# Column groups, packed samples and a reordered stream in a two-layer recurrent decoder step

## The chip, the cores and the metric

The kernel runs on one core of one Trainium2 chip, in one launch. The metric is the device time of that launch in microseconds, the median of several runs. The host only lays the arrays out.

## The reference

One inference step of a trunk of two layers (`DEPTH = 2`) for a prompt of 512 tokens and for 8 sample sequences of 4 tokens each, with the same weights. D_MODEL is 1024; there are 4 heads with keys and values of width 128; everything is float32.

```python
for l in range(DEPTH):
    mod = (silu(c) @ w_ada[l] + b_ada[l])              # 9 sequences x 6 * 1024: shifts, scales, gates
    h = rmsnorm(x, norm_mix[l]) * (1 + sc_m) + sh_m
    mix = token_mixers(h)                               # below
    x = x + gt_m * mix
    h = rmsnorm(x, norm_ffn[l]) * (1 + sc_f) + sh_f
    x = x + gt_f * swiglu(h)
y = rmsnorm(x, final_norm)

# token_mixers: one input projection, three branches of 4 heads, each with a 128 x 128 state a head
# A gated DeltaNet: width-4 causal convolution, SiLU, l2-normed q and k, per-head decay,
#   a triangular solve in each chunk; output rmsnorm, times silu(z)
# B retention: rotary q and k, fixed decays; output less its mean, divided by its deviation, times silu(g)
# C HGRN2: per-channel forget gate; output rmsnorm, times sigmoid(g)
# each branch projected to 1024, merged by sigmoid gates, and one output projection
```

The outputs are y for both groups and the new states of all branches and sequences.

## The kernel before

**Layout.** The 544 tokens (512 of the prompt, 32 of the samples) are columns, in two halves of 272: 256 prompt columns and 16 sample columns each. Features are on partitions.

**The stream.** The weights of all projections come as *slabs* of 128 output columns, in one order that `stream()` writes out by hand: rows, 12 convolution tiles, 8 rope tiles (q and k of retention), ret_v, gdn_z, ret_g, the gates and branches of the merge with the HGRN2 tiles between, output projection, feed-forward. Each slab is split by GpSimd (lines 600 and 602) into a high and a low part. A *k-step* (`k_tile`, line 627) is six TensorE matmuls: three products of parts, for two halves. A tile is 8 k-steps (branch tiles 4). Results go to two alternating PSUM buffers (`gemm_psum`), and ScalarE or VectorE works them off.

**Fills.** All small work runs between k-steps. Every engine walks through the same program with its own `Feed`: where TensorE's program has `fill(n, limit)`, n k-steps are issued, and ScalarE's and VectorE's programs have the same call, in which they work off the tiles that those steps complete. `drain(limit)` does the rest up to a limit (`Z_END`, `RG_END`, `M0_END` and so on). Each engine runs its program strictly in order. SyncE issues all transfers, in order too; it runs some slabs ahead.

**Conditioning.** The first 2 x 1024 columns of w_ada come as four groups of 2 MB; `silu_c` (9 columns) is the stationary operand, 512 columns stream, and 16 transposes turn the result (lines 769, 774). The other 32 tiles are computed in the convolution part with the weights as the stationary operand and 9 moving columns (`ada_tile`, line 790), three tiles per convolution tile (`ADA_STEPS`), from 4 buffers (`ADA_SLOTS`).

**Norms of heads.** `square_sum` (line 669) sums squares over partitions with a one-hot stationary operand of 8 columns into 8 rows; ScalarE takes the root, VectorE the reciprocal (`rows_of`, line 1231), and `spread` (line 678) spreads each row back over 128 partitions with 8-row weights; VectorE multiplies a tile at a time (line 1311 or 1405).

**Chunks and samples.** Each branch takes the prompt in four chunks of 128 tokens, in two pairs for gated delta, and then the samples (`c == NCH`), which have their own shapes: 32 columns a head. `gdn_level` does one of seven levels of the triangular inverse for a pair of chunks: masked columns on VectorE (`gdn_columns`), a fill, a second product (line 851), VectorE's additions (`gdn_add`, line 1491), transposes (line 858). `LEVEL_FILL` sets the k-steps in a level. For the samples, `sample_outputs` reads the 8 x 4 states with one matmul for each state (lines 703, 723: 8 or 4 moving columns), and `sample_states` makes the state updates from 32-row operands, a head at a time (line 735), which VectorE adds (line 1371). `out_norm` strings these together at the end of each branch: sums, two heads' states, spreads, the other two heads' states.

**Semaphores.** PSUM has four more banks (`mix_psum`) for the small work. `acquire(b)` waits until bank b is free, and VectorE or ScalarE releases it.

## Time and profile before

| | |
|---|---|
| median of 3 runs | 3214.1 us (3212.15 to 3222.64) |
| profiled execution | 3212.13 us |
| its span, first to last instruction | 3210.2 us |
| TensorE matmul busy | 2922.2 us, 91%, 20570 recorded |
| TensorE weight loads busy | 2681.7 us, 84% |
| VectorE, ScalarE, GpSimd busy | 1228.9, 472.3, 1400.5 us |
| mean granted TensorE clock | 0.903 of 2.4 GHz |
| bytes moved by DMA | 264.11 MB, 82 GB/s on average |

A matmul's busy time overlaps that of its neighbours, so that the mean duration of one is longer than what it adds; busy time of a group divided by its count is nearer to that. Line 1725 is the helper through which ScalarE records most of its work. "[idle before <-X]" is the time that an engine stood still before a row, and what ended it. Layer 0 runs from about 18 to 1605 us, and layer 1 repeats it.

### The profile page before, as it was taken

The numbers are of one execution on the slowest core, as the hardware profiler recorded it, in microseconds if no ns is written. First come the engines' busy times: TensorE is split into PE (matmuls) and PEld (weight loads), VectorE is DVE, ScalarE is ACT, GpSimd is POOL, SyncE is SP. The second block draws the span as 40 slices with busy tenths as digits, with TensorE's granted clock in tenths as the row PEclk, the third lists the DMA queues.
The fourth block names the chain that finished last, engine by engine and source line by source line (L and its number), as shares of the span: only waits on it lengthen the run. The fifth ranks groups of instructions, "written<-read, shape, count | busy, mean of one in ns | idle before, by whom it ended". The sixth has DMA issues, their size and how long they took to land. (4 is left out here: it accounts for less than half of the span.)

```text
span 3210.2 us, 48470 instructions
## 1 busy us (share of the span) xinstructions
PE 2922.2 (91%) x20570; PEld 2681.7 (84%) x20570; DVE 1228.9 (38%) x1572; ACT 472.3 (15%) x944; POOL 1400.5 (44%) x728
## 2 busy tenths in 40 slices
PE   6998998889998879999889989989899988799997
PEld 3977896877995879999859779968689968799996
DVE  2545412313353384333235444132225335732332
ACT  2221122111112110000023111221110121100000
POOL 1322232343533547776523222313355336477774
PEclk9987897986997989999999789969889979899998
DMA  7520011211411312222275100112113113122222
GB/s 276 183 88 27 27 47 40 83 56 40 121 45 43 114 60 91 83 91 85 63 266 172 57 27 28 53 50 59 56 60 112 47 37 127 60 90 82 93 80 74
DMA packets 126319, 264.11 MB, mean 82 GB/s; under 512 B 9616, under 2 KB 68496, under 8 KB 124304
## 3 DMA queue, kind: packets, MB, share of 16 engines
q1 hardware_dynamic: 126096, 260.93, 25.5%
q8 instruction: 165, 2.70, 0.3%
q14 instruction: 58, 0.48, 0.0%
HBM read 239.72 MB, written 21.17 MB: 81 GB/s over the span
## 5 line engine op out<-in xcount | busy, mean ns | idle before, releaser
L627 PE MATMUL gemm_psum<-h_hi_lo,w_hi_lo 128*128 128x272 f32 x12000 | 1710.9, 302 | 66.2 <-DVE h_hi_lo L1114 38.8
L627 PEld LDWEIGHTS gemm_psum<-h_hi_lo,w_hi_lo 128*128 128x128 f32 x12000 | 1619.4, 199 | 176.7 <-issue 139.8
L600 POOL TENSOR_TENSOR w_hi_lo<-w_raw,consts 128x1024 fp32r<-128x1024 f32 (+3 forms) x362 | 617.4, 1706 | 1744.5 <-PE gemm_psum L627 1618.8
L602 POOL TENSOR_TENSOR w_hi_lo<-w_raw,w_hi_lo 128x1024 fp32r<-128x1024 f32 (+3 forms) x362 | 784.0, 2166 | 28.4
L1725 ACT ACTIVATE tiles<-gemm_psum 128x544 f32<-128x544 f32 (+1 forms) x188 | 116.3, 623 | 1304.8 <-PE gemm_psum L627 1303.6
L627 PE MATMUL gemm_psum<-ffn_hi_lo,w_hi_lo 128*128 128x272 f32 x2112 | 266.8, 288 | 0.0
L627 PEld LDWEIGHTS gemm_psum<-ffn_hi_lo,w_hi_lo 128*128 128x128 f32 x2112 | 266.4, 188 | 0.0
L627 PE MATMUL gemm_psum<-o_hi_lo,w_hi_lo 128*128 128x272 f32 x1152 | 161.0, 296 | 16.3 <-POOL w_hi_lo L602 16.3
L627 PEld LDWEIGHTS gemm_psum<-o_hi_lo,w_hi_lo 128*128 128x128 f32 x1152 | 152.4, 194 | 18.1 <-POOL w_hi_lo L602 17.4
L1708 DVE TENSOR_TENSOR tiles<-gemm_psum,tiles 128x544 f32<-128x544 f32 x44 | 31.9, 725 | 319.6 <-PE gemm_psum L627 319.6
L1714 DVE TENSOR_TENSOR ffn_hi_lo<-tiles,ffn_hi_lo 128x544 fp32r<-128x544 f32 x44 | 119.8, 2722 | 1.5
L790 PEld LDWEIGHTS mix_psum<-silu_c,tiles 128*128 128x128 f32 x1024 | 120.1, 192 | 0.0
L790 PE MATMUL mix_psum<-silu_c,tiles 128*128 128x9 f32 x1024 | 118.3, 252 | 0.0
L1275 DVE SCALAR_TENSOR_TENSOR scratch<-scratch,params 128x568 f32<-128x568 f32 x72 | 102.1, 1418 | 2.6
L678 PE MATMUL mix_psum<-rows,consts 8*128 8x272 f32 x160 | 82.5, 667 | 21.1 <-DVEq L1057 21.1
L1725 ACT ACTIVATE scratch<-mix_psum 128x512 f32<-128x512 f32 (+3 forms) x90 | 48.5, 562 | 313.7 <-PE mix_psum L858 222.0
L1126 DVE TENSOR_TENSOR gated_sample<-gemm_psum,mod 128x32 f32<-128x32 f32 x48 | 9.2, 192 | 201.7 <-PE gemm_psum L627 201.7
L735 PE MATMUL mix_psum<-tiles 32*128 32x512 f32 x64 | 61.3, 1054 | 23.9 <-ACT tiles L1725 23.9
L1273 DVE TENSOR_SCALAR scratch<-scratch,params 128x568 f32<-128x568 f32 x24 | 30.8, 1283 | 132.6 <-ACT scratch L1725 132.2
L678 PEld LDWEIGHTS mix_psum<-rows,consts 8*128 8x128 f32 x160 | 45.0, 308 | 40.3 <-DVEq L1057 23.0
L1169 DVE TENSOR_TENSOR tiles<-gemm_psum,tiles 128x544 f32<-128x544 f32 x32 | 23.0, 718 | 139.7 <-PE gemm_psum L627 139.7
L1725 ACT ACT_TABLE_LOAD x44 | 56.5, 1283 | 123.3 <-issue 83.3
(225 smaller groups left out, 2413.2 us busy)
## 6 DMA issues: line engine op xcount, KB each, us to landing
w_raw<-in_w_gu SPq DMA_DIRECT2D x88, 512.0 KB, 3.5
tiles<-in_w_ada SPq DMA_DIRECT2D x64, 512.0 KB, 4.1
w_raw<-in_w_merge SPq DMA_DIRECT2D x48, 384.0 KB, 3.0
w_raw<-in_w_first SPq DMA_DIRECT2D x34, 512.0 KB, 3.6
w_raw<-in_w_ret SPq DMA_DIRECT2D x32, 512.0 KB, 3.4
w_raw<-in_w_hg SPq DMA_DIRECT2D x32, 512.0 KB, 3.5
w_raw<-in_w_merge SPq DMA_DIRECT2D x48, 256.0 KB, 2.7
w_raw<-in_w_dn SPq DMA_DIRECT2D x32, 384.0 KB, 3.1
```

The source lines that it names most:

```text
L600: pool.tensor_tensor(hi, src, ones[:, 0:1].broadcast_to([P, words]), ALU.mult).then_inc(hi_done, 1)
L602: pool.tensor_tensor(lo, src, hi.bitcast(F32), ALU.subtract).then_inc(split_done, 1)
L627: mm = pe.matmul(GP[:, 2 * (tile % 2) + h, 0:HALF], whl[:, n % 2, a, j * P:(j + 1) * P], rhs[:, b, step, h * HALF:(h + 1) * HALF], start=s ...
L678: pe.matmul(B[:, b, 0:HALF], sel[0:8, i, :], RWO[0:8, h * HALF:(h + 1) * HALF], start=True, stop=True).then_inc(full[b], 1)
L735: pe.matmul(B[:, 2 + half, :], ke[0:SW, h, :], UM[n][h % 2][0:SW, 4 * half:4 * half + 4, :], start=True, stop=True).then_inc(full[2 + half ...
L790: mm = pe.matmul(B[:, 2, j * NJ:(j + 1) * NJ], w[:, kk, :], CS[:, kk, :], start=kk == 0, stop=kk == KD - 1)
L1169: k.link(dve.tensor_tensor(halves(dst), gp(tile), halves(sg), ALU.mult))
L1273: ins = dve.tensor_scalar(co[:, 0:COW], xin, wt, None, ALU.mult)
L1275: ins = dve.scalar_tensor_tensor(out=co[:, 0:COW], in0=xin, scalar=wt, in1=co[:, 0:COW], op0=ALU.mult, op1=ALU.add)
L1708: k.link(dve.tensor_tensor(halves(FT[:, 1, :]), gp(tile), halves(FT[:, 0, :]), ALU.mult))
L1714: k.link(dve.tensor_tensor(AH[:, 1, i, :], FT[:, 1, :], AH[:, 0, i, :].bitcast(F32), ALU.subtract))
L1725: return act.activation(out, in_, func, **kw)
```

## The change

**Conditioning in column groups.** `silu_c` is padded with zeros to 32 columns. `conditioned` writes the eight products of a tile to four groups of 32 PSUM partitions in turn, which are four column groups of the array, with the weights as the moving operand. For the four first groups and for the 32 later tiles the four partial results of each group are copied to SBUF by ScalarE (`ada_copy`, three tiles at a time) and summed and turned by one product with a constant (`join`; `ada_join`). `ADA_SLOTS` is 7, of which 3 are loaded only after the first norm is done.

**Sums and spreads.** `four_sums` has 32-column one-hot weights, four heads in four column groups; `four_spreads` has 32-row weights, four heads in four row groups, one half of the tokens at a time, into four banks. VectorE multiplies four heads of one half at a time. The scale of q moves from `rows_of` into that product.

**Packed samples.** The 4 x 32 sample columns of the heads are one set of 128 columns: `nh` is 1 instead of 4 heads of 32, and masks keep the heads and sequences apart. `read_states` has the 32 columns of a head as the stationary operand and streams four states (512 columns), four heads in four column groups; ScalarE copies that to SBUF, and `pick` takes the right columns out with eight products of 16 moving columns. `sample_states` does four heads at a time in four row groups.

**Order.** gdn_z comes before ret_v in the stream, and `Z_END` lies before ret_v. `LEVEL_FILL` is (1, 1, 1). VectorE's additions come before the fills in `gdn_level`. In `out_norm` all sums, the root and the spreads come before all state updates. Buffers move accordingly (`sq_l2`, `sq_o`, `swap_temp`, `UM`, `QS`).

```diff
-LEVEL_FILL = (2, 1, 1)
-GATE_TURN = 10
+LEVEL_FILL = (1, 1, 1)
+GATE_TURN = 11
...
+    block("gdn_z", "first", 13, 4)
     block("ret_v", "ret", 8, 4)
-    block("gdn_z", "first", 13, 4)
     block("ret_g", "ret", 12, 4)
...
-Z_END = BASE["ret_g"]
+Z_END = BASE["ret_v"]
...
-    ADA_SLOTS = 4
+    ADA_SLOTS = 7
+    ADA_EARLY = 4
...
-    ADA_STEPS = (1, 4, 6)
+    ADA_STEPS = (3, 5, 6)
...
+                    if n == 0:
+                        sp.wait_ge(sig("h_ready"), KD)
+                        for j in range(ADA_EARLY, ADA_SLOTS):
+                            load_ada(j)
...
+                def four_sums(sq, j, first, last):
+
+                    if first:
+                        acquire(0)
+                        acquire(1)
+                    k.next(sig("square_ready"), H)
                     for h in range(2):
...
+                        for i in range(H):
+                            mm = pe.matmul(B[32 * i:32 * i + 32, h, 0:HALF], hot[:, j, :], sq[i][:, h * HALF:(h + 1) * HALF],
+                                           start=first, stop=last, skip_group_check=True)
+                    if last:
+                        mm.then_inc(sig("sums_done"), 1)
+
+                def four_spreads(j, half):
+
+                    for i in range(H):
+                        acquire(i)
+                        pe.matmul(B[:, i, 0:HALF], spr[32 * i:32 * i + 32, j, :],
+                                  RWO[32 * i:32 * i + 32, half * HALF:(half + 1) * HALF], start=True, stop=True
+                                  ).then_inc(full[i], 1)
...
+                def read_states(bank, queries):
+
+                    for half in range(2):
+                        acquire(bank + half)
+                        for h in range(H):
+                            mm = pe.matmul(B[32 * h:32 * h + 32, bank + half, :], queries[:, h * SW:(h + 1) * SW],
+                                           S8[:, h, 4 * half:4 * half + 4, :], start=True, stop=True, skip_group_check=True)
+                        mm.then_inc(full[bank + half], 1)
+
+                def pick(out, read, fresh):
+
+                    o4 = out.rearrange("p (h b t) -> p h b t", h=H, b=NS)
+                    for b in range(NS):
+                        mm = pe.matmul(o4[:, :, b, :], read[:, b, :], pick_seq[:, :, b, :], start=fresh,
+                                       stop=fresh or b == NS - 1, skip_group_check=True)
+                    return mm
...
-                def sample_states(n, h, limit):
+                    read_states(0, flat(0))
+                    fill(3, limit)
+                    k.peek(free[0])
+                    k.peek(free[1])
+                    acquire(2)
+                    pe.matmul(hcol(2, 0), val, sc, start=True, stop=False, skip_group_check=True)
+                    pick(hcol(2, 0), QS[n][0], False).then_inc(full[2], 1)
+
+                def sample_states(n, half):
 
                     ke = (small, rsm, hsm)[n]["kend"]
-                    k.next(sig("masked_values"))
-                    for half in range(2):
-                        acquire(2 + half)
-                        pe.matmul(B[:, 2 + half, :], ke[0:SW, h, :], UM[n][h % 2][0:SW, 4 * half:4 * half + 4, :],
-                                  start=True, stop=True).then_inc(full[2 + half], 1)
-                        fill(1, limit)
+                    if half == 0:
+                        k.next(sig("masked_values"))
+                    for h in range(H):
+                        p0 = 32 * h
+                        acquire(h)
+                        pe.matmul(B[:, h, :], ke[p0:p0 + 32, 0, :], UM[n][p0:p0 + 32, 4 * half:4 * half + 4, :],
+                                  start=True, stop=True).then_inc(full[h], 1)
...
-                    for i in range(H):
-                        square_sum(i, H, hot[:, i, :], 8, sq_o[n])
-                        fill(1, limit)
-                    for h in range(2):
-                        sample_states(n, h, limit)
+                    fill(2, limit)
+                    four_sums(sq_o[n], 0, True, True)
+                    fill(3, limit)
                     k.next(sig("rows_ready"))
-                    for i in range(H):
-                        spread(i, i)
+                    for half in range(2):
+                        four_spreads(0, half)
                         fill(2, limit)
-                    for h in range(2, H):
-                        sample_states(n, h, limit)
-
+                    fill(1, limit)
+                    for half in range(2):
+                        sample_states(n, half)
+                        fill(4, limit)
+
+
+                def conditioned(bank, at, w):
+                    for kk in range(KD):
+                        p0 = 32 * (kk % 4)
+                        mm = pe.matmul(B[p0:p0 + 32, bank, at], CS[:, kk, :], w[:, kk, :], start=kk < 4, stop=kk >= 4,
+                                       skip_group_check=True)
+                    return mm
...
+                def ada_join(g):
+                    k.next(sig("ada_lot_copied"))
+                    if g == 0:
+                        acquire(2)
+                    for j in range(g * ADA_LOT, min((g + 1) * ADA_LOT, 4 * KD)):
+                        o = j % ADA_LOT * P
+                        mm = pe.matmul(B[:, 2, j * NJ:(j + 1) * NJ], ada_part[g % 2][:, o:o + P], join, start=True, stop=True)
+                    mm.then_inc(sig("ada_lot_joined"), 1)
...
                 def gdn_level(chunks, lv, limit):
                     for c in chunks:
                         gdn_columns(c, lv)
-                    fill(LEVEL_FILL[0], limit)
                     if lv:
                         for c in chunks:
                             gdn_add(c, lv)
+                    fill(LEVEL_FILL[0], limit)
+                    if lv:
                         fill(LEVEL_FILL[1], limit)
                     fill(LEVEL_FILL[2], limit)
...
+                def ada_copy(g):
+                    count = min(ADA_LOT, 4 * KD - g * ADA_LOT)
+                    act.wait_ge(sig("ada_used"), g * ADA_LOT + count)
+                    if g >= 2:
+                        act.wait_ge(sig("ada_lot_joined"), g - 1)
+                    k.link(f(ada_part[g % 2][:, 0:count * P], B[:, 3, 0:count * P], ACT.Copy))
```

## Rows read from the trace of the kernel before

**Rows 1.** The page: TensorE's busy time, and its granted clock in 40 slices.

```profile
PE 2922.2 (91%) x20570; PEld 2681.7 (84%) x20570; DVE 1228.9 (38%) x1572; ACT 472.3 (15%) x944; POOL 1400.5 (44%) x728
...
PEclk9987897986997989999999789969889979899998
```

**Rows 2.** Line 627 (projections) by stretch, layer 0: busy (count), clock, DMA share, GB/s.

```profile
20.80:64.70 43.90, 0.01 (x1) 0.04 (x1) 0.97 0.76 300
74.90:213.60 138.70, 81.46 (x572) 73.55 (x571) 1.00 0.47 156
222.00:254.90 32.90, 16.16 (x60) 13.92 (x60) 0.50 0.05 17
254.90:465.80 210.90, 95.70 (x590) 83.86 (x590) 0.91 0.10 31
479.50:515.70 36.20, 18.53 (x116) 16.12 (x115) 0.86 0.13 42
515.70:573.80 58.10, 20.46 (x90) 17.29 (x90) 0.62 0.17 48
632.30:691.70 59.40, 40.84 (x301) 39.55 (x300) 0.91 0.19 58
691.70:772.00 80.30, 38.92 (x164) 33.58 (x165) 0.62 0.10 30
772.00:849.20 77.20, 77.20 (x618) 77.19 (x617) 1.00 0.27 84
949.80:980.20 30.40, 16.84 (x122) 16.47 (x121) 0.83 0.21 61
980.20:1048.50 68.30, 32.35 (x156) 27.95 (x155) 0.70 0.12 35
```

**Rows 3.** TensorE by line and form, both layers: count, busy us, mean duration in ns.

```profile
L678 PE MATMUL mix_psum<-rows,consts 8*128 8x272 f32 x160 | 82.5, 667 | 21.1 <-DVEq L1057 21.1
L735 PE MATMUL mix_psum<-tiles 32*128 32x512 f32 x64 | 61.3, 1054 | 23.9 <-ACT tiles L1725 23.9
...
L723 PE MATMUL mix_psum<-sample_cols,x 128*128 128x4 f32 x256 | 43.1, 300 | 0.0
...
L769 PE MATMUL mix_psum<-tiles,silu_c 128*9 128x512 f32 x64 | 27.8, 592 | 0.0
...
L703 PE MATMUL mix_psum<-scratch,x 128*128 128x8 f32 x128 | 22.0, 309 | 0.0
...
L669 PE MATMUL mix_psum<-tiles,consts 128*8 128x272 f32 x48 | 14.0, 417 | 2.5 <-ACT tiles L1725 2.5
```

**Rows 4.** All engines while the first conditioning weights arrive.

```profile
30.00:40.00 10.00, 10.00 (x26) 2.17 (x25) 8.40 (x9) 1.86 (x3) 0.00 (x0) 1.00 1.04 418
```

**Rows 5.** DMA issues by line: count, KB each, median us to landing.

```profile
scratch<-in_w_ada_first SPq DMA_DIRECT2D x4, 2048.0 KB, 19.4
```

**Rows 6.** TensorE in order of time, in the convolution stretch.

```profile
79.69 1.85 PE L790 MATMUL mix_psum<-silu_c,tiles 128*128 128x9 f32 x16
81.39 1.75 PE L627 MATMUL gemm_psum<-h_hi_lo,w_hi_lo 128*128 128x272 f32 x12
```

**Rows 7.** TensorE by line, 259 to 262 us.

```profile
L823 PE MATMUL mix_psum<-scratch,consts 4*128 4x128 f32 x32 | 2.8, 283 | 0.0
```

**Rows 8.** Order of time, a level of the first gated-delta pair.

```profile
287.80 2.89 DVE L1148 TENSOR_TENSOR tiles<-tiles,consts 128x544 f32<-128x544 f32 x1
...
291.83 1.97 PE L858 MATMUL mix_psum<-consts,scratch 128*128 128x128 f32 x8 [3.60 <-DVE scratch L1491]
```

**Rows 9.** VectorE by line and form, both layers.

```profile
L1275 DVE SCALAR_TENSOR_TENSOR scratch<-scratch,params 128x568 f32<-128x568 f32 x72 | 102.1, 1418 | 2.6
...
L1231 DVE RECIPROCAL rows<-rows 8x544 f32<-8x544 f32 x8 | 28.3, 3539 | 2.9 <-DVE x L1371 2.0 <-DVE x L1366 1.0
...
L1371 DVE SCALAR_TENSOR_TENSOR x<-x,scratch,mix_psum 128x128 f32<-128x128 f32 x64 | 18.0, 343 | 49.0 <-PE mix_psum L735 49.0
...
L1311 DVE TENSOR_TENSOR tiles<-mix_psum,tiles 128x544 f32<-128x544 f32 x16 | 11.6, 724 | 34.7 <-PE mix_psum L678 34.0 <-DVE tiles L1311 0.6
```

More of the change, by code:

```diff
@@ L1357, in sample_outputs, with sample_states @@
                     release(2)
[L1359 to L1360 removed]
+                def sample_states(n, half):
+                    if half == 0:
                         k.next(sig("states_landed"), 16 * H)
[L1362 to L1363 removed]
+                    eg = flat(12) if n == 2 else small["eg"][:, 0, :]
+                    for h in range(H):
+                        k.next(full[h])
                         if n == 1:
```

595 lines of the change are left out of this document (322 added, 273 removed).

## The prediction

> **What bounds the kernel.** I read the page first: TensorE is busy 91% of the span, no other engine over 44%, and the clock row dips wherever TensorE's share dips [rows 1]. So the sum is TensorE's, and what matters is which of its time is not the projections. I then asked for the projections alone (line 627), stretch by stretch through the first layer [rows 2]. The reader is to see the stretch from 772.0 to 849.2 us: nothing but projections, 77.2 us for 616 to 618 matmuls, 0.1255 us each at the full granted clock (2.4 GHz). With that price every other stretch splits into projections (count x 0.1255) and a rest: small products, waits, and projections at the half clock (1.2 GHz). The rests, in us: start 43.8; convolution 138.7 - 71.8 = 66.9; spreading of the norms 32.9 - 7.5 = 25.4; gated-delta pairs 210.9 - 74.0 = 137; their samples 21.6; the three output norms 46.8, 59.7, 48.7; the stretches with the retention and HGRN2 sample outputs 21.6 and 15.1. The projections themselves do not change, so the change is worth what it takes out of these rests, twice (the second layer repeats the first). The small products are priced by [rows 3], dividing busy time by count; each fp32 product is two recorded matmuls (a conditioning tile of eight calls shows x16 [rows 6]).
>
> **Start.** Four groups of conditioning weights, in all 64 recorded 512-column matmuls a layer, of 0.434 us each (27.8/64 [rows 3]), 27.8 us. Serial on one column group, that is 30.4 to 57.6. With the eight products dealt to four column groups, 7 us of work remain, and the weights decide: transfers ran at 418 GB/s [rows 4], the late groups landed a median 19.4 us after issue [rows 5], which from issues near 20 us puts the last at 40 to 43 us. Then 1.8 us of products, the copy 0.6, and 16 joining products with 128-column weights, 32 x 0.106 = 3.4 us (6.8 at the half clock) where 1.1 us of 9-row ones stood. The first projection comes near 55.5 instead of 64.7: **9 us** (serial: -2.5; at best 11).
>
> **Convolution.** An old conditioning tile is 16 recorded matmuls, 1.70 us from its start to the next projection [rows 6]; 32 of them 54.4 us, the eight sums of squares some 8 (32 recorded of 0.25 to 0.29 [rows 3]), and 4.5 is left. A new tile streams 128 columns with 32-column weights. Bounds: one column group after another costs the 1.76 us of 16 x 0.11 as 128-column products do; four at once 0.43. I take 0.65, since small matmuls are not issued endlessly close (an estimate). Adding 11 joins of 0.85 (64 x 0.106 and the switch) and two packed sums of 1.2: 4.5 + 20.8 + 9.4 + 2.4 = 37, so 66.9 becomes 37; the reciprocal without its scaling pass takes 1.5 us from the wait at the end. **31 us** (serial -13; best 37). What runs beside it: VectorE's four convolution passes, 4 x 1.42 = 5.7 us a tile [rows 9], under 8.7 us a tile on TensorE; ScalarE gets a 0.6 us copy; SyncE must bring 2 MB per tile, 240 GB/s, where this stretch moved 156 [rows 2] and 418 was reached [rows 4]. Seven slots give the transfers two tiles of lead.
>
> **Do packed products overlap?** Nothing here packs columns. But the gate products (line 823, four rows, at partitions 0 and then 32) pack rows by accident: 32 recorded matmuls in 2.8 us [rows 7], 0.088 each, where 128 columns cost 0.106 on a single group: at each change of row group the next group's begin before the last ones end. So row groups do run at the same time in fp32; for columns it is an inference.
> The Trainium skill, "TensorE: Matmul & The Clock Gate", Part 3, states that both overlap, 2.38x for three column tiles and 3.07x for four row tiles; no run here shows the column figure. At 2.38/3 of ideal a tile would cost 0.54 us instead of 0.65, 4 us a layer better.
>
> **Spreading.** Eight spreads with 8-row weights, 2.1 us each at the half clock, alternate with eight pairs of k-steps at half clock: 0.50 granted throughout [rows 2, 3]. New: four rounds of four row-packed products, 1.1 us at half clock (0.5 at full), and VectorE's multiply of 1,088 columns, 1.45 us (twice 0.724 [rows 9]). Its first rope tile (4.3 us: 2.89 for the sine product [rows 8] and two passes of 0.72) now falls between the third and fourth multiply, so the branch starts some 18.5 us after the first spread, not 33. **14 us** (4 to 20).
>
> **Gated-delta pairs.** VectorE worked off a rope tile between the masked columns and the additions; TensorE's transposes waited 3.60 us for the additions, then ran at the half clock [rows 8]. Four such waits and their slow stretches cost about 28 us of the 137; 888 other matmuls x 0.107 = 95 are unchanged. The additions now come first, so rope delays only the next level's columns, 5 us away. By counting k-steps (one fill less per level, ret_v moved behind gdn_z): rope 1 at step 16 stalls as before, 2 at step 24 and 7 at step 64 end in the last fill and still cost 4 + 3 each, 3 costs 2 to 3, the others nothing. SiLU of gdn_z puts table loads before ScalarE's copies, 3 us. **8 us** (-10 to 25).
>
> **Samples of gated delta.** State reads load 128-column weights for 8 moving columns, 64 recorded, 11 us a layer [rows 3], over 12 with the value products between. New: 16 products of 512 moving columns in column groups, 3.4 us (14 serial), 16 picks 3.4, and small products of 0.22 instead of 0.4 to 1.0. Four ScalarE copies of 0.6 lie under the fill. The drain of 18 k-steps ahead moves behind, so turn and gates meet VectorE cold: 2 us of wait. 21.6 becomes 15: **7 us** (-4 to 10). Retention and HGRN2, 43.1/4 = 10.8 us of reads each [rows 3] and 2 more of value products and slow clock, become 1.7 + 1.9: **19.5 us** for both (9.5 to 21).
>
> **Output norms.** The old order let VectorE do two heads' states before the 3.54 us reciprocal [rows 9], so spreads waited 4 us, eight 32-row state products took 0.96 [rows 3] at the half clock (16 recorded, 15 us), four spreads 8.4, four sums 4 to 5, and the k-steps between ran slow; the first norm also ran out of projections (4.9 us idle). New rest of norm 0: wait for four squares 0.5, sums 1.1, wait for root and reciprocal 2.4 (4.7 less three k-steps), two spread rounds 1.1, two state rounds 1.9, a wait for VectorE's 16 state updates of about 0.28 (duration 0.343 [rows 9], overlapping) before the second round 4.5, slow clock and switches 4.5: 16. Norm 1 adds 3.2 for its means and 4 where VectorE meets hg_f's forget gate: 24. Norm 2: 20. Gains 31 + 36 + 29 = **96 us** (60 to 108).
>
> **Sum.** 9 + 31 + 14 + 8 + 7 + 19.5 + 96 = 184.5 a layer, 369 in all. The profiled execution took 3212.1 us (span 3210.2), 0.1% under the median 3214.1. Forecast 2843, say **2845**; its own range, from the bounds that belong to overlapping groups, 2790 to 2890.
>
> **Rivals.**
> *Column groups do not overlap.* They still stream at full pace: 0.18 instead of 0.07 us for each of 720 recorded matmuls a layer, 81 us back, 3005. For it: no row shows them; against: row groups do. Chance 0.12.
> *Half overlap, or transfers bound the convolution.* Two at a time costs 35 us a layer, 2914. If the conditioning weights come no faster than this stretch's 156 GB/s, its 30 us go, 2905. Against: 418 was reached. Together 0.12.
> *The half clock stays.* If short packed groups between k-steps hold 1.2 GHz as the old norms do (0.62 [rows 2]), 20 k-steps a norm cost 15 instead of 4 us more, and the spreading 6: 39 a layer, 2922. Against: TensorE's unfilled share falls. Chance 0.12.
> *Slower: every column-group matmul pays its whole duration,* because the array empties between groups. At 0.283, 0.417 and 0.592 us by width [rows 3, 7] that is 0.35 on average, 203 us a layer more than I charge: 3249. It decides from 0.33 us a matmul on. Against: the sums of squares, eight-column weights between k-steps, cost 0.29 us a recorded matmul with their changes [rows 3], not their duration 0.417; streaming takes 0.227, so a change costs some 0.1. Chance 0.03.
> The Trainium skill, "TensorEngine Tiling (Array Packing)", Key Properties, says that changing the tiling mode drains TensorE; at the 0.1 us a change derived above it is inside my terms, once per matmul it is this rival.
>
> **Chances.** Forecast 0.55; the three middle rivals 0.36; slower 0.03; no change 0.01, if the waits merely move to VectorE; below 2790 0.05. Runs here tell 0.3% from no change. Range 2790 to 2960: out are slower, no change, the low tail and most of the serial case. Faster 0.96, same 0.01, slower 0.03.
>
> **What will show it.** Conditioning products starting in fours within some ns, a tile in 0.5 to 0.7 us; the first projection near 55 us; convolution rest near 37; the clock row above 0.93; norm stretches with rests of 16 to 24 and VectorE's state updates as the releaser before the second state round. Wrong if tiles take 1.7 us (serial), if TensorE waits for `tiles` transfers, or if the waits for line 1491's additions stay at 3.6 us.

## The result, and the profile after

The changed kernel took **2858.1 us** (median of 4 runs, 2855.1 to 2862.8) against 3214.2 for the kernel before on the same chip; the ratio is 0.8889, 95% interval 0.8868 to 0.8910. The forecast was 2845 (2790 to 2960), faster. The profiled execution took 2855.1 us, 357.0 less than that of before, where the sum of the prediction had 369.

The page first: TensorE's busy time and its granted clock, as in [rows 1].

```profile
PE 2567.6 (90%) x20358; PEld 2443.5 (86%) x20358; DVE 1224.0 (43%) x1537; ACT 442.8 (16%) x824; POOL 1402.6 (49%) x728
...
PEclk8998999999998989999979898999999998999998
```

TensorE lost 355 us of busy time with only 212 fewer recorded matmuls, 1% of them: what went is duration, not count. VectorE's busy time hardly moved (1228.9 to 1224.0). The clock row has fewer dips; the mean over the span is 0.946.

Next the projections alone (line 668 after, 627 before), by stretch of the first layer. Columns: stretch, its length, busy time (count), granted clock, DMA share, GB/s. They answer to [rows 2].

```profile
20.80:61.50 40.70, 0.00 (x0) 0.81 0.84 331
73.60:178.40 104.80, 81.79 (x566) 1.00 0.58 197
184.50:202.90 18.40, 9.68 (x60) 0.87 0.14 44
202.90:403.40 200.50, 82.30 (x504) 0.92 0.09 27
403.40:432.90 29.50, 21.45 (x138) 0.94 0.15 40
432.90:481.70 48.80, 35.95 (x259) 0.93 0.23 73
591.30:630.00 38.70, 25.67 (x172) 0.96 0.23 62
833.60:870.00 36.40, 20.68 (x133) 0.81 0.15 44
630.00:695.00 65.00, 65.00 (x521) 1.00 0.30 90
```

The last row gives the same price as before, 65.00/521 = 0.125 us. The first norm now covers itself with 259 projections at clock 0.93, where [rows 2] had 90 at 0.62.

To compare the layers, both traces were cut at the same events of TensorE (first projection, first spread, first transpose of the branch, first gate product of the samples, first sum of squares of a norm) and count x 0.1255 us of projections taken off each piece. What is left is the rest, in us per first layer:

| piece | rest before | rest after | gain | forecast |
|---|---|---|---|---|
| start, to the first projection | 64.7 | 61.55 | 3.2 | 9 |
| convolution, to the first spread | 77.6 | 43.3 | 34.3 | 31 |
| spreading | 25.5 | 10.9 | 14.6 | 14 |
| gated-delta pairs | 136.9 | 137.2 | -0.3 | 8 |
| samples of gated delta | 22 | 12 | 10 | 7 |
| retention and HGRN2 with their sample outputs | | | 19.6 | 19.5 |
| output norms 0, 1, 2 | 46.9, 59.7, 45.8 | 16.5, 17.0, 19.7 | 99 | 96 |

The pieces sum to 180. From projection 4200 on the two traces stay 179.4 us apart until the layer ends; the forecast was 184.5, and the second layer gave 177. The start's two figures include idle time that both kernels have. The stretches of retention and HGRN2 were not tested by a run of their own; in the trace the state reads of retention, which with their value products took TensorE 11.9 us in the kernel before (637.0 to 648.9 us), have become reads of 1.9 and picks of 1.7 us, near the forecast (1.7 and 1.9).

The new and changed products by form, both layers (count | busy us, mean ns | idle before, releaser), beside [rows 3].

```profile
L828 PE MATMUL mix_psum<-tiles,silu_c 128*32 128x128 f32 x1024 | 41.3, 279 | 0.0
...
L731 PE MATMUL mix_psum<-rows,consts 32*128 32x272 f32 x160 | 21.0, 539 | 19.7 <-DVEq L1146 17.1 <-DVEq L1141 2.5
L799 PE MATMUL mix_psum<-tiles 32*128 32x512 f32 x64 | 19.5, 739 | 3.9 <-DVEq L1141 3.8
...
L828 PE MATMUL mix_psum<-scratch,silu_c 128*32 128x512 f32 x64 | 11.9, 883 | 12.5 <-DMA scratch<-in_w_ada_first 12.5
...
L749 PE MATMUL mix_psum<-x,sample_cols 128*32 128x512 f32 x64 | 7.7, 598 | 0.0
```

The column-group products of a tile have a mean duration of 279 ns each, but 1,024 of them occupy only 41.3 us, 40 ns apiece: they lie over one another. One tile in order of time:

```profile
75.96 0.64 PE L828 MATMUL mix_psum<-tiles,silu_c 128*32 128x128 f32 x16
76.54 1.01 PE L668 MATMUL gemm_psum<-h_hi_lo,w_hi_lo 128*128 128x272 f32 x6
```

Sixteen recorded matmuls in 0.58 us from the first one's start to the next projection, against 1.70 in [rows 6]. Each break in the projections for a tile costs another 0.19 us (6 of them take 0.94 us instead of 0.75); the breaks for the old tiles cost 0.09 (12 take 1.60 us instead of 1.51).

### The profile page after: what moved, and what is told of

It is laid out like the page before. It is cut to its first block and busy times, and to the rows that moved or that the text cites. A ratio compares the mean times of both kernels' runs of the same rounds, so it can differ in the third digit from the quotient of the medians.

```text
span 2853.3 us, 47939 instructions
## 1 busy us (share of the span) xinstructions
PE 2567.6 (90%) x20358; PEld 2443.5 (86%) x20358; DVE 1224.0 (43%) x1537; ACT 442.8 (16%) x824; POOL 1402.6 (49%) x728
## 5 line engine op out<-in xcount | busy, mean ns | idle before, releaser
L668 PE MATMUL gemm_psum<-h_hi_lo,w_hi_lo 128*128 128x272 f32 x12000 | 1638.3, 296 | 75.5 <-DVE h_hi_lo L1203 46.7
L668 PEld LDWEIGHTS gemm_psum<-h_hi_lo,w_hi_lo 128*128 128x128 f32 x12000 | 1566.1, 194 | 127.5 <-issue 90.5
L668 PEld LDWEIGHTS gemm_psum<-o_hi_lo,w_hi_lo 128*128 128x128 f32 x1152 | 150.8, 192 | 20.2 <-POOL w_hi_lo L643 19.9
L1833 ACT ACTIVATE scratch<-mix_psum 128x512 f32<-128x512 f32 (+3 forms) x112 | 59.2, 547 | 410.1 <-PE mix_psum L947 196.6
L1833 ACT ACTIVATE tiles<-mix_psum 128x512 f32<-128x512 f32 (+1 forms) x78 | 43.6, 573 | 219.4 <-PE mix_psum L740 98.5
L940 PE MATMUL mix_psum<-scratch 128*128 128x64 f32 x388 | 51.5, 290 | 16.9 <-DVE scratch L1584 16.9
L1425 DVE COPY sample_cols<-tiles 128x128 f32<-128x128 f32 x20 | 9.5, 533 | 132.4 <-ACT tiles L1833 87.0
L940 PEld LDWEIGHTS mix_psum<-scratch 128*128 128x128 f32 x388 | 50.2, 208 | 18.2 <-DVE scratch L1584 18.2
L1218 DVE TENSOR_TENSOR x<-x,gated_sample 128x32 f32<-128x32 f32 x48 | 58.9, 1227 | 1.6
```

The lines of the kernel that those rows point to most:

```text
L668: mm = pe.matmul(GP[:, 2 * (tile % 2) + h, 0:HALF], whl[:, n % 2, a, j * P:(j + 1) * P], rhs[:, b, step, h * HALF:(h + 1) * HALF], start=s ...
L940: per_head(b0 + 1, lambda h: pe.matmul(columns(b0 + 1, h), t["u"][:, h, :], t["x"][:, h, :].rearrange("p (n t) -> p n t", t=m), start=True ...
L1218: k.link(dve.tensor_tensor(sample(xi), sample(xi), SCT[:, :].rearrange("p (a b) -> p a b", a=2), ALU.add))
L1425: k.link(dve.tensor_copy(SMP[:, at * H:(at + 1) * H, :].rearrange("p i (a b) -> p i a b", a=2), brt[:, src:src + H, :].rearrange("p i (a b ...
L1833: return act.activation(out, in_, func, **kw)
```

## Experiments

Times are medians; the ratio is to the kernel before, with its 95% interval. The changed kernel stands at 2858.1, ratio 0.8889 (0.8868 to 0.8910). In the diffs minus is the changed kernel. The rests below are cut at the same events in all kernels, norm 0 to the first projection of the next stage and norm 1 from 12 us ahead of its sums, so they stand 1 to 2 us above those of the table; among kernels that leave a norm and the fills alone they differ by 1 to 2 us (norm 0 18.3 to 20.3, norm 2 19.7 to 21.3). Over a whole layer two traces can drift further apart without a cause that I know: slots_4, whose time is that of the changed kernel, is 5.6 us behind it at the end of its first layer. The intervals of store_later, rope_last and states_first overlap that of the changed kernel slightly, but the slowest of their four runs each (2850.4, 2851.0, 2850.7) is under the fastest of its four (2855.1).

| kernel | us | ratio | against 2858.1 |
|---|---|---|---|
| one_group | 2957.5 | 0.9200 (0.9185 to 0.9215) | +99.4 |
| two_groups | 2889.7 | 0.8991 (0.8976 to 0.9006) | +31.6 |
| slots_4 | 2859.4 | 0.8891 (0.8875 to 0.8907) | +1.4 |
| split_waits | 2859.3 | 0.8900 (0.8885 to 0.8915) | +1.2 |
| store_later | 2848.9 | 0.8858 (0.8842 to 0.8874) | -9.1 |
| adds_late | 2857.0 | 0.8888 (0.8873 to 0.8903) | -1.1 |
| fill_211 | 2841.8 | 0.8843 (0.8828 to 0.8858) | -16.3 |
| fill_211_late | 2876.7 | 0.8955 (0.8940 to 0.8970) | +18.6 |
| rope_last | 2844.7 | 0.8861 (0.8846 to 0.8876) | -13.4 |
| states_first | 2849.7 | 0.8864 (0.8850 to 0.8879) | -8.4 |
| rows_serial | 2871.0 | 0.8928 (0.8912 to 0.8944) | +12.9 |
| best (four edits) | 2825.2 | 0.8790 (0.8778 to 0.8802) | -32.9 |

### Do column groups overlap? one_group, two_groups

```
-  p0 = 32 * (kk % 4)
-  mm = pe.matmul(B[p0:p0 + 32, bank, at], ..., start=kk < 4, stop=kk >= 4,
+  p0 = 32 * (kk % 1)                            # one_group; % 2 in two_groups
+  mm = pe.matmul(B[p0:p0 + 32, bank, at], ..., start=kk < 1, stop=kk >= 7,
```

Copies and joins were cut to the 32 or 64 rows that are written.

> All eight conditioning products of a tile go to column group 0 (the same 32-column weights, the same order; copies and joins on 32 rows), so none can overlap another. Theory: the four column groups overlap. A tile then goes from 0.57 us (16 recorded matmuls, 36 ns apart) to 16 x 0.11 = 1.76 us, +1.2 us on each of 32 tiles = +38 us a layer; in the start a group of 512 columns goes from 1.8 to 16 x 0.434 = 6.9 us, +5 us behind the last landing. Together +43 a layer, 2858 + 86 = 2944. Rival: the gain of the convolution comes from the shorter weights and the order, not from overlap: tiles stay near 0.6 us and the time within 5 us of 2858.

> The eight products go to two column groups in turn. Theory: time goes by the number of groups. A tile takes half of 1.76 us plus an issue overhead, 0.95 us, +0.38 x 32 = +12 us a layer, the start +1.7: 2858 + 28 = 2886. Rival: what sets a tile of four groups is the issue rate of the matmuls (36 ns each), not the number of groups: then two groups cost little, tiles 0.6 to 0.75 us, under +12 us in all. Second rival: two groups do not overlap within one product's two passes: +86 as with one group.

The line of the tile products in one_group, then in two_groups:

```profile
L828 PE MATMUL mix_psum<-tiles,silu_c 128*32 128x128 f32 x1024 | 123.8, 274 | 0.0
```

```profile
L828 PE MATMUL mix_psum<-tiles,silu_c 128*32 128x128 f32 x1024 | 68.3, 276 | 0.0
```

The mean duration of one is the same in all three kernels, 274 to 279 ns; the time that all occupy together goes 123.8, 68.3, 41.3 us. From a tile's first product to the next projection it is 1.86, 1.00 and 0.57 us for one, two and four groups; for 32 recorded matmuls of 512 columns in the start 13.8, 6.9 and 3.6 us. So overlap is shown, and nearly full: 1.9 times with two groups, 3.3 times with four. The rivals of no overlap and of an issue rate that sets the time fall. One group cost more than expected, +99 instead of +86: the convolution's rest rose by 44 a layer and the first projection came at 68.0 instead of 61.55.

### Do transfers bound the convolution? slots_4

```
-    ADA_SLOTS = 7
+    ADA_SLOTS = 4
```

> Four slots for the conditioning weights instead of seven. Theory: a tile of the convolution takes 9.0 us and its three conditioning loads land in 4.9 us each at 240 GB/s, far under what the start reached, so one tile of lead is enough: within 4 us of 2858. Rival: transfers are near the bound and the seven slots are what hides them: each of 10 tiles waits 1 us or more, +20 us or more.

The convolution's rest stayed at 43.7 us. The transfers are hidden, with four slots as with seven.

### Why did the start give 3 us and not 9? split_waits, store_later

VectorE and GpSimd ahead of the first projection in the changed kernel, in order of time (start, length):

```profile
49.64 1.89 POOL L641 TENSOR_TENSOR w_hi_lo<-w_raw,consts 128x1024 fp32r<-128x1024 f32 x1 [49.19 <-DMA w_raw<-in_w_first]
51.61 2.34 POOL L643 TENSOR_TENSOR w_hi_lo<-w_raw,w_hi_lo 128x1024 fp32r<-128x1024 f32 x1
52.03 0.31 DVE L1298 TENSOR_TENSOR mod<-mix_psum,params 128x144 f32<-128x144 f32 x1 [11.62 <-PE mix_psum L843]
52.49 1.55 DVE L1168 SCALAR_TENSOR_TENSOR scale_gain<-mod,params 128x72 f32<-128x72 f32 x1 [0.15 <-DVE mod L1298]
53.91 1.89 POOL L641 TENSOR_TENSOR w_hi_lo<-w_raw,consts 128x1024 fp32r<-128x1024 f32 x1
...
54.18 1.96 DVE L1184 TENSOR_TENSOR work<-tiles,scale_gain 128x128 f32<-128x128 f32 x2
...
55.88 2.48 POOL L643 TENSOR_TENSOR w_hi_lo<-w_raw,w_hi_lo 128x1024 fp32r<-128x1024 f32 x1
56.18 2.52 DVE L1186 TENSOR_TENSOR work<-work,mod 128x128 f32<-128x128 f32 x2
```

The conditioning reached VectorE 8 us earlier than before, 52.03 instead of 59.99. But in the kernel before GpSimd had finished splitting the first two weight slabs by then; now it is in the middle. VectorE's 72-column operation takes 1.55 us where it took 0.23, and ends at 54.04, 0.09 after GpSimd's operation ends at 53.95; the next pair ends 0.3 after GpSimd's next one. From the conditioning to the first projection 9.5 us pass instead of 4.7.

The first try holds GpSimd back, the second lets it go first.

```
 # split_waits (GpSimd)
+                    elif n == 1:
+                        pool.wait_ge(sig("h_ready"), 1)
 # store_later (SyncE)
                 for i in range(4):
                     sp.dma_start(ada_group[i], w_ada_first[l, i])
+                load_slabs(2)
                 sp.dma_start(CONV0[:, :, :], conv_in[l])
                 sp.dma_start(y_out[:, :, :], X[:, :, :])
-                load_slabs(3)
+                load_slabs(3)      # the third waits for the first split
```

> GpSimd waits with the split of each layer's second weight slab until VectorE has the first part of the modulated input; all else as in the changed kernel. Theory: in the start VectorE's modulation (1.55 us for an operation that took 0.23 before, 0.98 for one of 0.25) is slow because GpSimd splits weights beside it, which did not coincide before. Without it the operations take their old durations from 53.9 us on, and the first projection comes at 57.7 instead of 61.55: -3.9 a layer, 2858 - 8 = 2850. Rival: the operations are slow for another reason (transfers landing, or their operands): first projection at 61.5 or later, since the second slab is split later: 2858 to 2868.

> SyncE issues the first two weight slabs ahead of the store of x and the convolution states, instead of behind them. Theory: the last conditioning weights land at 42.9 us and the first slab, 0.5 MB, only at 49.1, because the store of x (2.2 MB, 5 us) is in between; so GpSimd's split runs from 49.6 to 58.4, across VectorE's modulation that starts at 52.0. With the slabs at 44 to 45 GpSimd splits the first from 44 to 48.5 and the second from 48.5 to 52.8, VectorE's operations keep their old durations, and the first projection comes at 56 to 57 instead of 61.55: 2858 - 10 = 2848. Rival: the store slows the slabs in any order (shared queues): first projection at 60 or later, within 4 us of 2858. Second rival: the collision moves onto the later parts of the modulation as it did when GpSimd waited: first projection at 57, but the first tile ends where it did (73.7 us).

In split_waits the first projection came at 57.99, as expected, and the time did not change, which was nobody's forecast. The trace shows why:

```profile
57.16 0.68 DVE L1205 TENSOR_TENSOR h_hi_lo<-tiles,h_hi_lo 128x512 fp32r<-128x512 f32 x1
57.60 7.38 SPq L572 DMA_DIRECT2D x<-in_s_gdn  x3
57.92 1.90 POOL L643 TENSOR_TENSOR w_hi_lo<-w_raw,consts 128x1024 fp32r<-128x1024 f32 x1 [4.03 <-DVE h_hi_lo L1205]
57.96 2.14 DVE L1194 TENSOR_SCALAR tiles<-tiles,scale_gain,mod 128x512 f32<-128x512 f32 x1
...
57.99 1.70 PE L670 MATMUL gemm_psum<-h_hi_lo,w_hi_lo 128*128 128x272 f32 x6 [6.05 <-DVE h_hi_lo L1205]
59.90 2.40 POOL L645 TENSOR_TENSOR w_hi_lo<-w_raw,w_hi_lo 128x1024 fp32r<-128x1024 f32 x1
60.02 2.83 DVE L1205 TENSOR_TENSOR h_hi_lo<-tiles,h_hi_lo 128x512 fp32r<-128x512 f32 x1
...
62.90 0.59 PE L670 MATMUL gemm_psum<-h_hi_lo,w_hi_lo 128*128 128x272 f32 x1 [3.21 <-DVE h_hi_lo L1205]
```

The collision moved with the split: the same operation (line 1205) takes 0.68 us just ahead of GpSimd's and 2.83 beside it, and TensorE stops again for 3.21 us. In store_later GpSimd's fourth operation ends at 52.28, before the 72-column one begins, and that is back at 0.23:

```profile
49.93 2.35 POOL L644 TENSOR_TENSOR w_hi_lo<-w_raw,w_hi_lo 128x1024 fp32r<-128x1024 f32 x1
...
52.11 0.31 DVE L1299 TENSOR_TENSOR mod<-mix_psum,params 128x144 f32<-128x144 f32 x1 [11.34 <-PE mix_psum L844]
52.57 0.23 DVE L1169 SCALAR_TENSOR_TENSOR scale_gain<-mod,params 128x72 f32<-128x72 f32 x1 [0.15 <-DVE mod L1299]
```

The first slab landed at 43.2 instead of 49.2, the first projection started at 56.8, and the second tile's first conditioning product at 68.95 instead of 73.69: 4.7 us, which last to the end of the convolution; the time fell by 9.1. The trace doesn't show 4.7 us kept in each layer: at the end of the first layer the two kernels are level again, and the second layer's start is 6.9 us shorter (51.7 us without a projection instead of 58.6, where the kernels with the start unchanged have 55.5 to 58). The collision's price at the start is shown; that all of it reaches the end is not.

The Trainium skill, "SBUF — State Buffer", section "SBUF: two separate sides", says that VectorE and GpSimd have one pair of ports in common, taken as an exclusive lock for a whole instruction, which a VectorE operation needs when it runs in a two-port mode, or when it has two inputs in SBUF while GpSimd's reads SBUF too. The traces here agree: line 1298, which reads PSUM and SBUF, took 0.31 us beside GpSimd as without it, while line 1168, with two SBUF inputs, took 1.55 instead of 0.23.

### Why did the pairs give nothing? adds_late, fill_211, fill_211_late, rope_last

```
 # fill_211
-LEVEL_FILL = (1, 1, 1)
+LEVEL_FILL = (2, 1, 1)
 # adds_late (VectorE's gdn_level); fill_211_late has both
-                    if lv:
-                        for c in chunks:
-                            gdn_add(c, lv)
                     fill(LEVEL_FILL[0], limit)
                     if lv:
+                        for c in chunks:
+                            gdn_add(c, lv)
                         fill(LEVEL_FILL[1], limit)
 # rope_last (the stream of tiles)
-    block("rope", "ret", 0, 8)
     block("gdn_z", "first", 13, 4)
+    block("rope", "ret", 0, 8)
```

> VectorE's additions go behind the first fill again, LEVEL_FILL stays (1, 1, 1). Theory: by the count of k-steps no rope tile ends in a level's first fill under (1, 1, 1) (they end at steps 24 and 32 in pair 0 and 64 in pair 1, in the last and middle fills), so the order of the additions changes nothing: within 4 us of 2858. Rival (that of the prediction): early additions save some 4 us and 3 us of half clock for each rope tile: +15 us or more.

> LEVEL_FILL back to (2, 1, 1), additions still early. One k-step more between columns and additions in each of 14 levels a layer. Theory: time of the pairs is set by where rope tiles end. Four steps a level leave levels ending the rope tiles 2, 3 and 4 inside pair 0 (as in the kernel before), with early additions only one that ends in the last fill stalls. Additional fill covers nothing, because level chains already have cover: within 8 us of 2858, sign open (-8 to +8). Rival: a level needs more cover than one k-step: 10 us or more faster.

> LEVEL_FILL (2, 1, 1) and the additions behind the first fill, the arrangement of the kernel before, everything else new. Theory: the pairs' rest was 137 us before and is 137 us after, so this is worth nothing: within 6 us of 2858, with three stalls of 3.6 us at the transposes in pair 0 and none from rope in pair 1. Rival (the prediction): early additions and the shorter fill save 8 us a layer: +16 us.

> The stream puts the four gdn_z tiles ahead of the eight rope tiles (the changed kernel has them behind). Theory: the gated-delta pairs gained nothing because rope tiles that end in the last fill of a level hold up the next level's columns (3.8 us and some 3 us of half clock each). With gdn_z at steps 8 to 32, the stalls near 214, 241 and 269 us and their slow stretches go (7.5, 7 and 2 us), less about 3 us of table loads on ScalarE; the stall near 335 us stays: -11 to -14 a layer, near 2833. Rival: waits are set by the chain of a level itself and rope only fills them: within 5 us of 2858. Second rival: ScalarE's table loads before its copies cost as much as VectorE's rope: within 5 us or slower.

The first three with the changed kernel make a square of the two edits (us; in brackets the rest of the pairs in the first layer):

| | additions late | additions early |
|---|---|---|
| LEVEL_FILL (2, 1, 1) | 2876.7 (142.5) | 2841.8 (125.4) |
| LEVEL_FILL (1, 1, 1) | 2857.0 (137.5) | 2858.1 (137.2) |

Early additions are worth 35 us with four k-steps a level and nothing with three. The longest waits of the kind, from the views of waits (us in total, times, longest), first fill_211_late, then the changed kernel:

```profile
PE mix_psum L947 <- DVE scratch L1599: 21.6, 6, 3.6
```

```profile
PE mix_psum L940 <- DVE scratch L1584: 16.9, 6, 3.6
```

Line 947 is the transposes behind the additions (the waits of [rows 8]); line 940 is the second products of a level, behind its columns. In fill_211 neither line waits any more: a tile has eight k-steps and a level four (the first has three), so rope tiles end at the same place of a level, and it is one that early additions have cleared. With three k-steps a level they wander through it; in the first layer tiles 2 and 7 ended in the last fill and held line 940 for 3.60 us each, tile 3 for 1.24. Each full stall is followed by half clock:

```profile
246.07 2.76 PE L940 MATMUL mix_psum<-scratch 128*128 128x64 f32 x16 [3.60 <-DVE scratch L1584]
```

These 16 take 2.5 us to the next projection instead of 1.70.

The pairs' rest fell by 11.8 us a layer in fill_211, and the time by 16.3 in two layers, because some of it is lost again in norm 0, whose rest rose from 18.9 to 22.2. There VectorE's low part of the output (line 1529, two inputs in SBUF) now runs beside GpSimd's split; in the changed kernel, shown second, it doesn't:

```profile
434.83 6.19 DVE L1529 TENSOR_TENSOR o_hi_lo<-tiles,o_hi_lo 128x1088 fp32r<-128x1088 f32 x2 [0.54 <-DVE tiles L1514]
```

```profile
444.33 2.49 DVE L1529 TENSOR_TENSOR o_hi_lo<-tiles,o_hi_lo 128x1088 fp32r<-128x1088 f32 x2 [0.54 <-DVE tiles L1514]
```

My expectation for fill_211 ("within 8 us, sign open") and the zero for fill_211_late both missed; both times the number of the rival came. For fill_211 its reason, more cover, is not told apart from mine, the phase, by the time alone; the stalls that vanish are those that the count names. The expectation for adds_late held. Against fill_211_late, which has the old arrangement, the new one gained 18.6 us, but only 5.3 us a layer of it in the pairs; about as much again is norm 0, whose rest is 25.0 in fill_211_late. So the time came close to twice the forecast of 8, and the pairs did not. They gained nothing as a whole because in the kernel before 588 projections could cover them and now only 504 can, with three k-steps a level or with four, since ret_v was moved behind: with the old arrangement inside, the rest rose from 136.9 to 142.5. In that trace the projections are used up at 392.3 us, and for the last 16 us of the pairs TensorE has none; four waits of 0.69 us for ScalarE's copies and one of 1.15 for VectorE lie there, 3.9 us of the 5.6. That the shorter cover makes the whole rise was not tested by itself.

rope_last gave 13.4 of the expected 25 us. The pairs' rest fell from 137.2 to 130.6 and the spreading's from 10.4 to 7.3, because the rope tiles 0 and 1 no longer meet the start of the branch; but a rope tile in a late level still stalled once (3.60 us), and new waits came at the samples (rest 15.2 instead of 12.2).

### What makes the norms short? states_first, rows_serial

```
 # states_first: PE, out_norm (VectorE and ScalarE in the same order)
                     fill(3, limit)
+                    sample_states(n, 0)
+                    fill(4, limit)
                     k.next(sig("rows_ready"))
                     for half in range(2):
                         four_spreads(0, half)
...
-                    for half in range(2):
-                        sample_states(n, half)
-                        fill(4, limit)
+                    sample_states(n, 1)
+                    fill(4, limit)
 # rows_serial
-  pe.matmul(B[:, i, 0:HALF], spr[32 * i:32 * i + 32, j, :], RWO[32 * i:32 * i + 32, ...
+  pe.matmul(B[:, i, 0:HALF], spr[:, j, :], RWO[:, ...
-  pe.matmul(B[:, h, :], ke[p0:p0 + 32, 0, :], UM[n][p0:p0 + 32, ...
+  pe.matmul(B[:, h, :], ke[:, 0, :], UM[n][:, ...
```

> In the output norms the first half of the state products and VectorE's updates from them stand before the reciprocal and the spreads, as in the kernel before; all products keep their packed forms. Theory: a large part of the norms' gain is the order. Spreads then wait for root, 8 masked copies (2.5 us), two rounds of products (1.1), 16 updates (4.5) and the reciprocal (3.5), 12 us, of which 7 k-steps cover 5.3; against that the wait of the second round for the updates (3.8 us and its half clock) goes. Net +5 us and 3 us of half clock for norms 0 and 2, +2 for norm 1, +18 a layer: 2858 + 36 = 2894 (2875 to 2905). Rival: the packed forms alone make the gain: within 6 us of 2858.

> Spreads and sample state products contract over all 128 rows instead of 32, so that four in a row no longer run in different row groups (values of norms and sample states are then wrong by the other rows; the number and the columns of the matmuls stay). Theory: what shortened the norms is that products come in fours between waits, with VectorE's multiply over 1,088 columns, more than that they overlap: a spreading round goes from 0.74 to 1.0 us, a state round from 1.07 to 1.8, so +2 us a norm at full clock, 3 with the half clock, and +1.2 in the spreading of the convolution's norms: +8 to 10 a layer, 2858 + 18 = 2876 (2868 to 2885). Rival: the overlap makes the norms' gain: +30 a layer or more, above 2910.

My theory of the order fell: putting the state products ahead of the reciprocal made the kernel 8 us faster, not 36 slower. TensorE does wait longer for the reciprocal, as expected,

```profile
449.12 1.29 PE L731 MATMUL mix_psum<-rows,consts 32*128 32x272 f32 x8 [5.80 <-DVEq L1147]
```

5.80 us in norm 0 of states_first against 2.24 in the changed kernel. But it is one wait in place of two. In the changed kernel the second round of state products waits for VectorE's updates, bank by bank:

```profile
448.96 1.41 PE L799 MATMUL mix_psum<-tiles,scratch 32*128 32x512 f32 x4
449.29 3.66 DVE L1483 SCALAR_TENSOR_TENSOR x<-x,scratch,mix_psum 128x128 f32<-128x128 f32 x12 [0.15 <-DVE x L1483]
...
450.52 1.12 PE L799 MATMUL mix_psum<-tiles,scratch 32*128 32x512 f32 x2 [0.15 <-DVEq L1141]
...
451.79 1.99 PE L799 MATMUL mix_psum<-tiles,scratch 32*128 32x512 f32 x2
453.19 1.12 DVE L1483 SCALAR_TENSOR_TENSOR x<-x,scratch,mix_psum 128x128 f32<-128x128 f32 x4 [0.24 <-DVE x L1483]
...
453.71 8.52 PE L668 MATMUL gemm_psum<-h_hi_lo,w_hi_lo 128*128 128x272 f32 x48
```

Eight matmuls take 4.76 us, and 22 projections behind them run at the half clock. The rest of norms 0 and 1 came out alike in both orders (18.9 and 18.9, 18.5 and 19.5); norm 2 fell from 19.7 to 14.4. Not all of that need be the order: line 1529's pair of operations in norm 2 took 5.31 us beside GpSimd's split in the changed kernel and 2.49 in states_first, where GpSimd stands still, and the two were not told apart. So the order on its own is not where the 96 us came from.

rows_serial moved as expected in all (+12.9 for 18), though I had mis-sized its parts. Without row groups a spreading round takes 1.74 us instead of 0.74 to 0.95, and a state round 3.03 instead of 1.07, so the products of a norm cost some 6 us more. Yet the rests of norms 0 and 2 (20.2 and 19.6) lie among those of the kernels with packed rows; norm 1's rose from 18.5 to 22.4, and that of the spreading from 10.4 to 14.2, together 7.7 us a layer, where the time grew by 6.5. The slower products filled the time in which TensorE waited for VectorE's updates, and kept the clock up:

```profile
439.00:478.00 39.00, 36.66 (x238) 31.77 (x238) 17.65 (x37) 9.60 (x17) 17.71 (x9) 1.00 0.17 49
```

That is all engines in norm 0 of rows_serial (TensorE, weight loads, VectorE, ScalarE, GpSimd, clock, DMA): clock 1.00, where the changed kernel has 0.91 to 0.93. Overlap of row groups is therefore a small part of what the norms gained, 0 to 4 us of some 33 each. What is left as the cause is fewer rounds with more in each (two spreads over 1,088 columns instead of four over 544, two state rounds instead of four) and projections left to cover them; that remainder was not taken apart further.

### The edits that helped, together: best

> Four edits at once: LEVEL_FILL (2, 1, 1), gdn_z ahead of rope, the first half of the state products ahead of the reciprocal, and the store of x behind the first two slabs. Theory: they act at different places. Alone they gave -16.2, -13.4, -8.4 and -9.1 us against 2858. The first two share the stalls of the gated-delta pairs: under (2, 1, 1) no rope tile stalls a level, so gdn_z ahead only takes the stalls of rope 0 and 1 at the start of the branch (4.3 and 3.8 us and their half clock) and adds waits at the samples, -8. Sum 2858 - 16 - 8 - 8 - 9 = 2817 (2808 to 2826). Rival: the phase of the rope tiles against the levels shifts and new stalls of 3.6 us appear: 2826 to 2845.

2825.2 us is 1.2% under the changed kernel and 12.1% under the kernel before. It lies at the upper end of what was expected (2808 to 2826), 8 us above its middle. The sum of fill_211, states_first and store_later alone would be 2824: rope_last added nothing to them. The rival's mechanism is in the trace, on the second products of a level (line 942 here):

```profile
PE mix_psum L942 <- DVE scratch L1588: 17.2, 6, 2.9
```

With the four gdn_z tiles in front, three rope tiles a layer end in a level's last fill again, and the pairs' rest is 137.8.

## Why the prediction was right, point by point

**Where the time was.** Reading each stretch as projections at 0.1255 us and a rest held in the trace after: the projections' price did not change, and the gain sits in the rests. Convolution, spreading, samples and the norms taken together came within 4 us each of their forecasts. That the sum is closer than its worst terms is partly luck: start and pairs gave 14 us a layer less than forecast, and convolution, samples and norms 9 more.

**Overlap of column groups.** The 0.12 for no overlap and the 0.03 for a slower kernel rested on row groups that overlap by accident [rows 7]. The inference from rows to columns held. I took 0.65 us a tile, 0.57 was measured; tiles and joins together gave 34 instead of 31. A matmul in column groups costs 0.036 to 0.04 us, far from the 0.33 at which the slower case decided. By the figure of the Trainium skill, "TensorE: Matmul & The Clock Gate", Part 3, 2.38x for three column tiles, a tile would take 0.54 us (an estimate); the trace is near it, with 3.3 times for four groups, 0.82 of ideal. The drain at a change of tiling mode, which the Trainium skill states in "TensorEngine Tiling (Array Packing)", Key Properties, shows in this trace at most as the 0.19 us of each break.

**Start, 3 for 9.** The transfers went as forecast (last group landed at 42.9, forecast 40 to 43), and the joins took 4.7 us at both clocks, inside 3.4 to 6.8. The last group's products took 3.3 us and not 1.8: they stand behind a wait of 4.22 us for the transfer, and the clock granted to them was 0.57. What failed above all is a step that had no sentence: behind the joins I kept VectorE's 4.7 us of modulation from the kernel before. It took 9.5, since work that comes 8 us earlier now meets GpSimd's split. store_later shows the price, 4.7 us at the start.

**Pairs, 0 for 8, the term that was most off.** The stalls fell where the count of k-steps put them: 3.8 us near 219 us as before, 3.60 at steps 24 and 64, 1.24 at the third. The 28 us of four old waits was mis-sized as a saving: with the repeats that I listed (4 + 3 twice, 2 to 3), and the first one staying as it was, most of it was spent again. And I gave no price to the projections that the pairs lose with ret_v.

**Samples of gated delta, 10 for 7.** State reads and picks took 3.6 and 3.8 us, for 3.4 and 3.4. The 2 us of wait, where turn and gates would meet VectorE cold, did not come: TensorE has no wait between 403.4 and 433 us.

**Norms, 99 for 96, by other shares.** Norm 0 was 16.5 (forecast 16), with the wait for VectorE's updates at 3.7 us (4.76 less the 1.07 of the first round; forecast 4.5) and 2.3 us lost to slow projections behind it. Norm 1 was 17 instead of 24. VectorE does meet hg_f's forget gate, but TensorE waits only 1.74 us for it, ahead of the second spread round, where I had 4:

```profile
609.29 0.50 DVE L1249 TENSOR_SCALAR tiles<-tiles,lb_layer 128x544 f32<-128x544 f32 x1
609.70 1.28 DVE L1514 SCALAR_TENSOR_TENSOR tiles<-mix_psum,tiles 128x1088 f32<-128x1088 f32 x1
611.10 1.02 PE L731 MATMUL mix_psum<-rows,consts 32*128 32x272 f32 x8 [1.74 <-DVEq L1141]
```

And I had carried the 4.5 us of norm 0's state updates over to norm 1, whose updates are a few operations of 512 columns at 0.75 us (line 1478), so that its second state round takes 1.67 us, 0.6 more than its first. The order about the reciprocal, which I gave first among the reasons, is not where the gain comes from; states_first says so.

**The half clock.** It stayed only behind waits. The convolution and the retention norm ran at 0.96 to 1.00; norm 2 at 0.81, behind a wait of 4.06 us for its reciprocal.

## What to carry to other kernels

Small products in four column groups cost a third to a quarter of their serial time. Packing them pays where TensorE is what everybody waits for; where it would wait anyway, as in the norms, products without row groups cost almost nothing more. When an edit brings work forward, list what every other engine does at the new time, and carry over no duration from the old place. And when filler work is laid between the steps of a chain, count in which gap each filler item ends: one k-step more a level was worth 16 us here, and moving gdn_z ahead, which helped by itself, brought the stalls back together with it.

## What the runs showed of the hardware

VectorE's operations with two inputs in SBUF last until some 0.1 to 0.6 us behind the end of GpSimd's running operation: 0.23 to 1.55 us, 0.68 to 2.83, and one with a single SBUF tensor input and two columns of scalars (line 1194) 0.55 to 2.14. The same is inside the rope stalls. The sine product of a rope tile, all 16 of them in the changed kernel:

```profile
L1237 DVE TENSOR_TENSOR tiles<-tiles,consts x16: 707/2900/2922, 196.7 to 1747.8; 128x544 f32<-128x544 f32 x16
```

Shortest 707 ns, median 2900: 15 of them begin with GpSimd at work, and the one of 0.71 us (at 217.44) is the only one without. In the kernel before it is the same, 14 beside GpSimd at 2.89 to 2.94 us and two alone at 0.71. The end of a projection tile sets off both the rope work and GpSimd's split of the next slab, and the product then begins together with the split's second operation; in the stall near 246 us:

```profile
242.00 2.35 POOL L643 TENSOR_TENSOR w_hi_lo<-w_raw,w_hi_lo 128x1024 fp32r<-128x1024 f32 x1
242.03 2.89 DVE L1237 TENSOR_TENSOR tiles<-tiles,consts 128x544 f32<-128x544 f32 x1
```

The 2.89 us that the prediction took from [rows 8] as that product's duration is thus 0.7 us of work and 2.2 of waiting, the larger part of each 3.6 us stall. What a rope tile would cost with that operation away from the split was not run.

The granted clock fell behind waits of a few us, and came back while the projections ran: behind the second state round of norm 0, 22 projections took 5.1 us before it was at full again.
